# Second attention of a two-block transformer: every other round with its TensorE and VectorE work turned round

## What is computed

```
q = axial_rope(rms_norm(q, q_gain)); k = axial_rope(rms_norm(k, k_gain)); kc = rms_norm(kc, k_gain)
s = einsum('bqhgd,bshd->bhgqs', q_b, concat(kc, k)) * scale      # 16 query heads, 4 key heads, 512 keys
p = softmax(s); o = einsum('bhgqs,bshd->bqhgd', p, concat(vc, v))
y_lat = o @ w_o
```

## Time and profile before

| what | value |
|---|---|
| median of 3 runs | 1519.37 us (1518.77 to 1519.54) |
| profiled execution: span from first to last instruction, which is all of its own time that is on record | 1520.0 us |
| TensorE busy | 1504.8 us, 99% of the span |
| VectorE busy | 944.5 us, 62% |
| ScalarE busy | 714.6 us, 47% |
| granted TensorE clock, mean | 0.999 |
| second attention, from the first scores to the start of the output projection | 728.6 to 780.4 us of the span |

### The profile page before, as it was taken

The page is one execution under the profiler, slowest core; times in us unless marked ns, Lnnn a source line. Parts: engine busy times, 40 slices in busy tenths (PEclk is TensorE's granted clock), DMA queues, the critical chain, the costliest instruction groups (busy, mean ns, idle before and its releaser), DMA issues.

```text
span 1520.0 us, 21592 instructions
## 1 busy us (share of the span) xinstructions
PE 1504.8 (99%) x9007; PEld 1258.6 (83%) x9007; DVE 944.5 (62%) x1245; ACT 714.6 (47%) x1011; POOL 79.0 (5%) x104
## 2 busy tenths in 40 slices
PE   8999999999999999999999999999999999999998
PEld 6777767778888888879778888899888889988887
DVE  6532585553424342476977666679789856779973
ACT  5422585332213222345765545545656546556553
POOL 0220141000000000000010000034000000000000
PEclk9999999999999999999999999999999999999999
DMA  9766425452532232454255555656565554565652
GB/s 361 238 196 213 131 44 177 168 184 93 183 111 83 90 104 90 161 192 131 65 168 192 180 181 186 204 180 214 179 197 178 198 190 153 179 205 170 196 192 83
DMA packets 245298, 252.44 MB, mean 166 GB/s; under 512 B 17758, under 2 KB 238273, under 8 KB 245201
## 3 DMA queue, kind: packets, MB, share of 16 engines
q1 hardware_dynamic: 243648, 248.53, 50.2%
q0 software_dynamic: 944, 1.87, 0.3%
q10 hardware_dynamic: 608, 0.66, 0.1%
HBM read 248.94 MB, written 1.05 MB: 164 GB/s over the span
## 4 chain that ended last, share of the span: by engine, by line
PE 94%; DVE 3%; ACT 2%; DMA 0%; issue 0%; SPq 0%; DVEq 0%; ACTq 0%
PE psum L414 91%; PE psum L1014 3%; DVE wl L400 1%; ACT scr L1055 1%; DMA vtok<-in_ctx 0%; PE psum L985 0%; ACT wh L393 0%; DVE hT L2151 0%; PE psum L583 0%; DVE scr L2097 0%; DVE kl L1610 0%; DVE mix L2111 0%; ACT scr L694 0%; DVE sums L1125 0%; PE psum L2487 0%
## 5 line engine op out<-in xcount | busy, mean ns | idle before, releaser
L400 DVE TENSOR_TENSOR wl<-raw,wh 128x2048 fp32r<-128x2048 f32 (+1 forms) x183 | 413.6, 2262 | 223.6 <-ACT wh L393 223.4
L393 ACT ACTIVATE wh<-raw 128x2048 fp32r<-128x2048 f32 (+1 forms) x183 | 344.3, 1883 | 291.5 <-PE psum L414 285.9
L414 PE MATMUL psum<-x,wh 128*128 128x512 f32 (+1 forms) x1520 | 461.7, 364 | 0.0
L414 PE MATMUL psum<-x,wl 128*128 128x256 f32 x1312 | 367.5, 280 | 0.0
L414 PEld LDWEIGHTS psum<-x,wh 128*128 128x128 f32 x1520 | 271.6, 188 | 48.5 <-issue 1.3
L414 PEld LDWEIGHTS psum<-x,wl 128*128 128x128 f32 x1312 | 248.2, 189 | 0.0
L414 PE MATMUL psum<-xh,wh 128*128 128x512 f32 (+1 forms) x624 | 239.9, 384 | 0.3 <-DVE xl L765 0.3
L414 PE MATMUL psum<-xl,wh 128*128 128x512 f32 (+1 forms) x624 | 236.9, 380 | 0.0
L414 PE MATMUL psum<-xh,wl 128*128 128x512 f32 (+1 forms) x624 | 236.8, 380 | 0.0
L414 PEld LDWEIGHTS psum<-xh,wh 128*128 128x128 f32 x624 | 118.1, 189 | 29.2 <-DVE xl L606 4.3
L414 PEld LDWEIGHTS psum<-xh,wl 128*128 128x128 f32 x624 | 118.2, 189 | 22.1
(11 more groups left out here) (287 smaller groups left out, 2018.0 us busy)
## 6 DMA issues: line engine op xcount, KB each, us to landing
raw<-in_ffn_w_in SPq DMA_DIRECT2D x44, 1024.0 KB, 5.0
pre<-in_ada_w SPq DMA_DIRECT2D x26, 1024.0 KB, 9.7
raw<-in_ada_w SPq DMA_DIRECT2D x22, 1024.0 KB, 6.4
raw<-in_w_ffn_gate SPq DMA_DIRECT2D x22, 1024.0 KB, 5.2
raw<-in_w_ffn_up SPq DMA_DIRECT2D x22, 1024.0 KB, 5.2
raw<-in_w_ffn_down SPq DMA_DIRECT2D x19, 1024.0 KB, 4.8
raw<-in_ffn_w_out SPq DMA_DIRECT2D x16, 1024.0 KB, 4.8
raw<-in_na_w_qkv SPq DMA_DIRECT2D x10, 1024.0 KB, 5.9
```

The costliest lines, as they stand in the source:

```text
L393: act.e.activation(wh[:, c % NSPL, 0:z], raw[:, p % NRAW, 0:z], ACT.Copy).then_inc(W.hi, 1)
L400: dve.e.tensor_tensor(wl[:, c % NSPL, 0:z], raw[:, p % NRAW, 0:z], wh[:, c % NSPL, 0:z].bitcast(F32), ALU.subtract).then_inc(W.lo, 1)
L414: return pe.e.matmul(o, l, r, start=start, stop=stop, skip_group_check=shared)
```

## The change

In the second attention, rounds 5, 7, 9 and so on (`back`) run TensorE's steps in the opposite order: values first, then the turn, then the scores. To have the values ahead of the turn in those rounds, `before` in `steps1` becomes true for all groups. On VectorE the reversed rounds do reciprocals, spread and copy of unit i-2 ahead of the maxima of unit i. ScalarE's, GpSimd's and SyncE's orders stay as they are. The first attention has `back` false in every round and stays as it is. No instruction is added or removed.

```
     def __init__(self, ..., scores, turn, back):
...
-            for i in range(A_.last):
+            def score_pe(i):
                 if i < n:
                     ready(i)
                     if A_.scores[i] in A_.scores[:i]:
                         used = max(u for u in range(i) if A_.scores[u] == A_.scores[i])
                         pe.wait_ge(S.exp, b_.exp + 2 * used + 2)
                     score(i, bank[A_.scores[i]:A_.scores[i] + 2])
+
+            for i in range(A_.last):
+                if not A_.back(i):
+                    score_pe(i)
                 if i < 3:
                     behind_scores(i)
                 values_pe(i, True)
                 if 0 <= i - 2 < n:
                     turn_pe(i - 2)
                 values_pe(i, False)
+                if A_.back(i):
+                    score_pe(i)
...
+            for i in range(A_.last):
+                if spread_act and 0 <= i - 2 < n:
+                    recip(i - 2)
+                if A_.back(i):
+                    copy(i - 2)
+                    maxima(i)
+                else:
+                    maxima(i)
+                    copy(i - 2)
                 prep(i)
                 if i <= n:
                     behind_values(i)
...
-        steps1 = Steps([2 * g + 4 for g in range(8)], [2 * g + 5 for g in range(8)], [False] * 8, [2 * g + 5 for g in range(8)])
+        steps1 = Steps([2 * g + 4 for g in range(8)], [2 * g + 5 for g in range(8)], [True] * 8, [2 * g + 5 for g in range(8)])
...
-                       sums0, lambda j, h: rms1(j)[:, h:h + 1], rms1, lambda g: xh4[:, g, :], lambda g: xl4[:, g, :], SCORES1, 2)
+                       sums0, lambda j, h: rms1(j)[:, h:h + 1], rms1, lambda g: xh4[:, g, :], lambda g: xl4[:, g, :], SCORES1, 2,
+                       lambda i: i % 2 == 1 and i >= 5)
```

More of the change, by code:

```diff
@@ L83, with __init__ @@
 class Attention:
-    def __init__(self, S, base, units, groups, steps, pt, rb, wide, sums, scale, rms, hi, lo, scores, turn):
+    def __init__(self, S, base, units, groups, steps, pt, rb, wide, sums, scale, rms, hi, lo, scores, turn, back):
         self.S, self.base, self.units, self.groups, self.steps = S, base, units, groups, steps
         self.pt, self.rb, self.wide, self.sums, self.scale, self.rms, self.hi, self.lo = pt, rb, wide, sums, scale, rms, hi, lo
-        self.n, self.scores, self.turn = len(units), scores, turn
+        self.n, self.scores, self.turn, self.back = len(units), scores, turn, back
         self.last = 1 + max(steps.pv) + 2
@@ L1114, in recip, with maxima @@
                 dve.e.reciprocal(A_.sums[:, 2, at_:at_ + parts, :], A_.sums[:, 1, at_:at_ + parts, :]).then_inc(S.recip, 1)
-            for i in range(A_.last):
-                if spread_act and 0 <= i - 2 < n:
-                    recip(i - 2)
+            def maxima(i):
                 if i < n:
@@ L1131, in attention_dve, with copy @@
                 middle(i)
-                j = i - 2
+            def copy(j):
                 if 0 <= j < n:
@@ L1142, in attention_dve @@
                                           A_.sums[:, 2, at_:at_ + parts, :].unsqueeze(3).to_broadcast([P, parts, 2, 64])).then_inc(S.recip, 1)
-                    if i > n:
-                        behind_values(i)
+                    if j + 2 > n:
+                        behind_values(j + 2)
                     dve.wait_ge(S.turned, b_.turned + j + 1)
@@ L1147, in attention_dve @@
                     dve.e.tensor_copy(to, o).then_inc(S.copied_d, 1)
-                elif i > n:
-                    behind_values(i)
+                elif j + 2 > n:
+                    behind_values(j + 2)
+            for i in range(A_.last):
[7 more added lines that the diff above has]
+                    copy(i - 2)
                 prep(i)
@@ L1178, in program @@
         C0 = Attention(A0, A0._make([0] * len(A0)), units0, groups0_, steps0, pt0, rb0, wide0, sums0, lambda j, h: 1.0, None,
-                       lambda g: xh1[:, g // 2, side0(g)], lambda g: xl1[:, g // 2, side0(g)], SCORES0, 2)
+                       lambda g: xh1[:, g // 2, side0(g)], lambda g: xl1[:, g // 2, side0(g)], SCORES0, 2, lambda i: False)
         def score0(i, b):
```

## The result

The changed kernel takes **1523.72 us** (median of 21 runs, 1521.29 to 1527.35). The kernel before was run 21 times beside it: median 1521.06 us (1518.77 to 1524.55). The ratio is 1.0018, with a 95% interval of 1.0011 to 1.0024, so the change costs 2.7 us, between 1.7 and 3.6. The shift that was forecast, 2.3, lies in that interval. The absolute time lies outside the range, 0.12 us above its upper end and 2.0 above the forecast of 1521.7. Of these 2.0, 1.7 come from the base (1519.37 in three runs, 1521.06 in 21) and the rest from the shift.

A forecast was written before the change was run, and what follows sets the result against it. TensorE was taken to bound the kernel before, VectorE's line the new order: 2.0 us saved on TensorE, 4.3 given back in waits, +2.3 on the median 1519.37 gives 1521.7 us. The range was 1518.2 to 1523.6 us.

The forecast's parts named there:

- TensorE's own work: Second attention: joined groups of one kind and fewer junctions save TensorE 2.0 us, 5.76 a pair of rounds instead of 6.08.
- VectorE's line: Second attention: hand-overs from one odd turn to the next sum to 6.08 us; 1.6 lost in steady rounds.
- the 2.49: Item of VectorE's line: from M(i+1) to the end of C(i-1), 1.81 + 0.68 us, reciprocals and spread inside.
- `query_sin(3)` and `query_lo(3)`: VectorE's passes for the last queries, between maxima in rounds 5 and 9, stand in the line and cost 0.6 us each.
- ScalarE in round 8: `query_hi(3)` ahead of ScalarE's copy of unit 6 makes that copy later than VectorE's; T(7) loses 0.37 us.
- The end: Last rounds of second attention: C(15) no longer has half of the values as cover; some 1.1 us lost.
- bounds: Allowances for what no row shows, such as hand-overs, `query_lo(3)` and overlaps: shift of +1.3 to +3.3 us.
- From the projection on nothing changes: Behind the second attention the shift goes through unchanged; SyncE's later loads cost nothing, up to 3.3 us if cover went.
- The base: Whole kernel: the shift of 2.3 us is added to the earlier kernel's median of 1519.37 us.
- TensorE stays the bound: Rival, second attention: the saved junctions come through, -2.0 us, 1517.4 us; chance 11%.
- ScalarE closes the line: Rival, second attention: ScalarE, not VectorE, closes the line between odd turns; +3.05 us, about 1522.4 to 1524; chance 12%.
- Nothing comes of it: Rival: steady rounds equal, query passes and end fit into gaps; -0.8 to +0.8 us, 1519.4 us; chance 11%.

The follow-up runs named there:

- run 21: Not a label: the kernel before, unchanged, was run 21 times beside the changed kernel; median 1521.06 us (1518.77 to 1524.55).
- half the maxima: Changed kernel with second-attention maxima over the first 256 of 512 keys and queries' gain a 64th, timing only; V1(0) to projection 40.27 us, changed kernel 43.98.
- combination with copies first: Changed kernel with copy ahead of maxima in rounds 5 to 13, query passes moved, rounds 15 on as before; 1522.57 us, ratio 1.0002 to the kernel before.
- maxima first: Changed kernel with VectorE's old order, maxima of unit i ahead of the copy of unit i-2, TensorE's rounds still reversed; 1535.34 us.
- second values behind the turn: Changed kernel with only the values' second half put back: turn, values, scores in the reversed rounds; 1529.0 us.
- copy first in all rounds: Changed kernel with VectorE's copy of unit i-2 ahead of the maxima of unit i in every round from 5; V1(0) to projection 42.75 us, changed kernel 43.98.
- control with half the maxima: Kernel before, with maxima over 256 keys and queries' gain a 64th; V1(0) to projection 40.90 us, against 41.04 without the edit.
- spread on GpSimd: Changed kernel with the spread of the reciprocals of units 0 to 13 moved from VectorE to GpSimd; V1(0) to projection 42.58 us, changed kernel 43.98.

## Why the prediction was right and where it was wrong

- **TensorE's own work, -2.0.** Right in its parts. A pair without waits is 5.70 to 5.73 in the run with half the maxima (5.76 forecast); there the stage still holds waits around the query passes, so the 2.0 as a whole was seen in no run.
- **VectorE's line, 6.08 a pair.** Right in kind, 0.09 short. Item by item in the pair T(11) to T(13): 0.99 to S(13), 1.01 to M(13), 1.47 to M(14), **2.55** to the end of C(12), 0.15 to the turn, together 6.17. The step that was mis-sized is the 2.49: it came from unit 2, whose spread starts 0.19 behind the reciprocals. For even units from unit 4 on, which close the line here, the distance is 0.26 (771.22 to 771.48); their spread has one more wait, for the values of the group two before. The trace of before had it as well, at unit 8:

```profile
758.46 0.16 DVE L1114 RECIPROCAL sums<-sums 128x2 f32<-128x2 f32 x1
758.72 0.23 DVE L1141 COPY wide<-sums 128x128 f32<-128x128 f32 x1
```

  With some hundredths in the other items the pairs are 0.09 to 0.12 longer than forecast, 0.39 over four of them (the fifth is the next but one point).
- **`query_sin(3)` and `query_lo(3)`, 0.6 each.** Right: 6.83 and 6.77 against 6.17, and moving them brought it back.
- **ScalarE in round 8, 0.37.** Here 0.6 was lost against a pair of 6.08. The mechanism was right: ScalarE's copy closed T(7), at 752.66 + 0.59 = 753.25, VectorE's had ended at 753.05. What I could not know was the late product of unit 7 (+0.36), partly covered by closer passes and a hand-over of 0.10 instead of 0.14 (-0.14). The pair came out at 6.68 instead of 6.45, 0.23 more.
- **The end, about 1.1.** Right: T(13) to V1(7) is 7.61 us (772.45 to 780.06), 7.60 was forecast.
- **Together.** 43.98 against 43.34: 0.64 too little, 0.39 for the line and 0.23 for round 8. The sum stayed inside its bounds, +1.3 to +3.3, but neither of the two stood among the items that the bounds were made of, so that is in part luck.
- **From the projection on nothing changes.** Right, within 0.3: SyncE's loads come later and nobody waits for them.
- **The base.** This step failed and put the absolute time outside the range. I had added the shift to the median of three runs and taken their spread of 0.8 us for the spread of the kernel. 21 runs of the same kernel spread over 5.8 us and have their median 1.7 higher. The range was made of mechanisms only and had no term for this.
- **The rivals.** TensorE stays the bound: refuted, 0.40 to 1.04 us of idle time ahead of each odd turn from T(5) to T(13). ScalarE closes the line: refuted as given (only T(7) and the end), but it is the next bound, at 5.81 to 5.89, and shows as soon as VectorE is shortened. Nothing comes of it: refuted by the interval, which begins at +1.7. The change in time is 0.18%, at the edge of what I called distinguishable: "same" was given 72%.

The contention that the GPSIMD Engine Reference (Specifications) of the Trainium skill describes went the other way than I had allowed for. `query_lo(3)` took 0.93 us before, with GpSimd's pass (755.79 to 756.53) over its start at 756.14; in the changed kernel GpSimd's ended at 756.70, the query pass began at 756.82, and took 0.68. The trace agrees with the rule, and the new order avoids the meeting by 0.12 us, by chance. In the combination with copies first the chance went the other way and cost 0.50.

## What to carry to other kernels

Joining work of one kind on the busiest engine saves something only if the engine that feeds it has slack in the new order: add up the whole line of hand-overs from one turn of the shared buffer to the next, item by item, and compare it with what the pair takes today, before counting saved junctions. Do that for the even turns as well as for the odd ones: with the maxima first it was an even turn that closed the loop. Take the duration of each item from an instance with the same waits, not from the first of its kind. And when a few us in 1500 are the question, compare stages of two traces from a common start, and give the absolute time the spread of many runs, not of three.

## What the runs showed of the hardware

- **Half-speed stretches of TensorE.** In the stage they followed four of the eight waits of TensorE of 1.77 to 2.04 us (maxima first, second values behind the turn) and none of 1.26 us and less. One more, from about 694 us on, came in seven of the 13 profiled executions of the same instructions and not in the other six, and cost 1.5 us. TensorE's rows have no idle time ahead of it, but they show products of two columns there, nearly 2 us of them. From the kernel before:

```profile
692.02 1.93 PE L414 MATMUL psum<-cst,hs_t 128*128 128x2 f32 x16
693.81 0.43 PE L414 MATMUL psum<-xh,wh 128*128 128x256 f32 x1
```

  The products of 128x256 are 0.12 us apart before these (690.10 to 690.22) and 0.21 behind them (694.04 to 694.25). So rows without idle time don't exclude such a stretch. That the narrow products are its reason is not shown: six executions had them without it.
- **A pass of VectorE and one of GpSimd that meet.** Both have two inputs in SBUF, and in the five meetings seen the one that started second was held. `query_lo(3)` of the kernel before is one (0.93 us). VectorE's product of two columns took 0.70 us (copy first in all rounds, 763.68, GpSimd's pass 763.63 to 764.36), 0.66 (755.73, above) and 0.49 (half the maxima, 753.80, GpSimd's 753.55 to 754.28) instead of 0.16, and each time ended with GpSimd's pass to 0.02. In the control with half the maxima it was the other way round: `query_lo(3)` started first (753.32) and took its 0.68, and GpSimd's pass, from 753.50, took 1.10 instead of 0.74. Where VectorE's product began in the last 0.14 us of GpSimd's pass it took 0.16 as always (nine cases).
- **Slower products at a full clock.** In the execution with the spread on GpSimd the span is 1524.6 us although its stage is 1.4 shorter. Between 1087 and 1270 us it fell 3.3 us behind, with the clock recorded as full and no wait. One window of it, and then of the kernel before:

```profile
1200.00:1220.00 20.00, 20.00 (x115) 17.32 (x114) 15.21 (x17) 11.40 (x11) 0.00 (x0) 1.00 0.56 184
```

```profile
1200.00:1220.00 20.00, 20.00 (x117) 17.63 (x116) 14.70 (x13) 10.59 (x10) 0.00 (x0) 1.00 0.59 196
```

  Five of the profiled executions have this loss, the instructions there are the same in all, and its cause is open. With the half-speed stretch that makes 4.8 us, near the 5.8 by which runs of one kernel differ here; that these two are what the timed runs differ by is not shown.
- **A delay of 0.31 to 0.36 us at one place of VectorE's stream**, the 704th record in nine kernels, which doesn't show when a wait that is needed anyway has that place.
